# Forming the first expert pair's turned rows on the tensor engine, with idle transposes ahead of them

## The reference, cut to what matters

```python
s = sigmoid(ht @ w_router)                      # 512 tokens, 32 experts in 4 groups
g_idx = argmax(top_k(sel, 2)[0].sum(-1))        # best group, then two experts in it
...
xb = x_pad[tok]                                 # the tokens of one expert
hid = silu(xb @ w1[e]) * (xb @ w3[e])           # 1024 -> 512
ys = (hid @ w2[e]) * wt[:, None]                # 512 -> 1024
out = zeros.at[row_tok].add(ys)
```

## Time and profile before

| | |
|---|---|
| median of 3 runs | 800.81 us (800.76 to 807.31) |
| the profiled execution | 801.7 us |
| its span | 799.8 us |
| TensorE busy | 707.7 us (88%) |
| VectorE busy | 310.2 us (39%) |
| DMA engines, mean over the span | 327 GB/s, 261.22 MB |
| mean granted TensorE clock | 0.951 |

### The profile page before, as it was taken

One profiled execution on the slowest core, in us unless ns is written; L12 is line 12 of the kernel. 1 busy time (PEld: TensorE's weight loads), 2 busy tenths in 40 slices (PEclk: granted clock), 3 DMA queues, 4 the chain that ended last, 5 costly groups with the idle time before them and its releaser, 6 DMA issues.

```text
span 799.8 us, 9109 instructions
## 1 busy us (share of the span) xinstructions
PE 707.7 (88%) x3786; PEld 380.9 (48%) x3786; DVE 310.2 (39%) x555; ACT 176.2 (22%) x308; POOL 71.7 (9%) x68
## 2 busy tenths in 40 slices
PE   1899999796996589999976999999999998998994
PEld 0478778355685334434422444434444443453442
DVE  1172371479566522233304233333333323322326
ACT  4143362424134211101110011101101110110104
POOL 0007500119002010000000000000000000000000
PEclk9999999998898669999987899999999999999998
DMA  9990333896027919999998599999999999999972
GB/s 342 388 377 33 106 106 105 322 386 238 2 107 272 384 30 420 430 425 419 403 429 351 207 399 425 428 426 427 426 429 425 425 426 427 427 425 428 428 306 105
DMA packets 38857, 261.22 MB, mean 327 GB/s; under 512 B 4002, under 2 KB 4386, under 8 KB 26016
## 3 DMA queue, kind: packets, MB, share of 16 engines
q1 hardware_dynamic: 34560, 250.64, 76.5%
q0 software_dynamic: 2480, 6.16, 2.1%
q10 hardware_dynamic: 1776, 3.84, 1.3%
HBM read 260.76 MB, written 4.20 MB: 331 GB/s over the span
## 4 chain that ended last, share of the span: by engine, by line
PE 49%; DMA 12%; DVE 5%; ACT 1%; issue 1%; DVEq 0%; SPq 0%
PE bank L819 23%; DMA ring<-in_w 12%; PE bank L828 11%; PE bank L836 3%; PE bank L837 2%; PE bank L808 2%; DVE x L1492 1%; PE bank L793 1%; PE bank L811 1%; PE bank L860 1%; PE bank L801 1%; PE bank L845 1%; PE bank L869 1%; DVE x L1589 1%; PE bank L758 1%
## 5 line engine op out<-in xcount | busy, mean ns | idle before, releaser
L819 PE MATMUL bank<-ring,low 128*64 128x512 f32 x1024 | 231.8, 607 | 13.7 <-DMA ring<-in_w 10.8
L819 PEld LDWEIGHTS bank<-ring,low 128*64 128x64 f32 x1024 | 77.7, 140 | 158.0 <-issue 156.9
L1492 DVE TENSOR_TENSOR x<-x,bank 128x512 f32<-128x512 f32 x136 | 84.1, 681 | 84.5 <-PE bank L837 83.7
L828 PE MATMUL bank<-ring,low 128*64 128x512 f32 x512 | 113.4, 595 | 0.9 <-DVE x L1492 0.9
L828 PEld LDWEIGHTS bank<-ring,low 128*64 128x64 f32 x512 | 36.2, 137 | 66.1 <-issue 64.4
L1482 DVE SCALAR_TENSOR_TENSOR y_raw<-bank,keep,g2b 128x512 f32<-128x512 f32 x32 | 24.0, 751 | 88.4 <-PE bank L828 88.4
L1660 POOL DMA_INDIRECT xg_rows<-x_rows,keep x16 | 16.3, 1019 | 440.4 <-PE bank L793 423.2
L836 PE MATMUL bank<-y_hi,slot_tok 128*128 128x512 f32 x128 | 53.8, 420 | 0.2 <-DVE y_lo L1487 0.2
L1542 DVE TENSOR_TENSOR low<-low,bank 128x512 f32<-128x512 f32 x16 | 11.0, 687 | 110.1 <-PE bank L819 110.1
L1246 DVE TENSOR_TENSOR w_lo<-ring,w_hi 128x512 fp32r<-128x512 f32 x48 | 33.4, 712 | 51.8 <-ACT w_hi L1033 51.8
L837 PE MATMUL bank<-y_lo,slot_tok 128*128 128x512 f32 x128 | 50.6, 395 | 0.0
(11 more groups left out here) (242 smaller groups left out, 817.0 us busy)
## 6 DMA issues: line engine op xcount, KB each, us to landing
ring<-in_w SPq DMA_DIRECT2D x99, 2048.0 KB, 20.9
ring<-in_w_mod SPq DMA_DIRECT2D x12, 2048.0 KB, 15.2
ring<-in_w_in SPq DMA_DIRECT2D x4, 2048.0 KB, 22.5
ring<-in_w_out SPq DMA_DIRECT2D x2, 2048.0 KB, 12.7
x<-in_x SPq DMA_DIRECT2D x4, 512.0 KB, 6.4
after<-in_b_mod POOLq DMA_DIRECT2D x1, 2048.0 KB, 8.3
x_rows<-mid ACTq DMA_DIRECT2D x4, 512.0 KB, 15.4
out<-x SPq DMA_DIRECT2D x4, 512.0 KB, 2.6
```

The source lines that it names most:

```text
L819: last = mm(bk[e * CAP:(e + 1) * CAP, :], xb[:, k, e * CAP:(e + 1) * CAP], unit(n % SLOTS, KD)[:, k, :], start=k == 0, stop=k == KD - 1)
L828: last = mm(bk[e * CAP:(e + 1) * CAP, :], hid_t[:, k, e * CAP:(e + 1) * CAP], unit(n % SLOTS, KF)[:, k, hf * 512:(hf + 1) * 512], start=k ...
L1492: return v.tensor_tensor(acc[:, t, c], acc[:, t, c], bk[:, :], ALU.add)
```

## The change

`first_rows_turned` multiplies, for each of the eight pieces k and each token tile t, the piece of `h2` (stationary, every eighth column) by `onehot` (moving) and adds over t in PSUM. The result is what `turn_rows` would leave in G0 and G1 for pair 0: rows picked and transposed at once. It is placed after `p_ready` 1 and before `slots_to_partitions` of pair 0. `turn(0)` and gather 0 go; the gathers start with pair 1 and their counts shift by one. `keep_busy(n)` issues n transposes of `ident` into the bank of job hT20, whose contents have been read: 24 before TensorE waits for `chosen`, 8 before it waits for `p_ready` 1.

```diff
@@ -766,7 +766,16 @@
             logits(NT - 2)
             logits(NT - 1).then_inc(job_done, 1)
 
+            idle_bank = bank[JOB["hT20"] % 8]
+            assert len({JOB[n] % 8 for n in ("hT20", "lg", "rk", "cnt")}) == 4
+
+            def keep_busy(n):
+
+                for _ in range(n):
+                    nc.tensor.transpose(idle_bank[:, 0:P], ident, ident)
+
             b = start("rk")
+            keep_busy(24)
             pe.wait_ge(chosen, 1)
             for t in range(NT):
                 for u in range(t + 1):
@@ -878,17 +887,28 @@
             def turn(q):
-                pe.wait_ge(gath, 16 * q + 16)
+                pe.wait_ge(gath, 16 * q)
                 turn_rows()
 
+            def first_rows_turned():
+
+                for k in range(KD):
+                    g = (G0, G1)[k // 4]
+                    for t in range(NT):
+                        by_k = h2[:, t, :].rearrange("s (p k) -> s k p", k=KD)
+                        last = mm(g[:, (k % 4) * P:(k % 4 + 1) * P], by_k[:, k, :], onehot[:, t, :], start=t == 0, stop=t == NT - 1)
+                    if k % 4 == 3:
+                        last.then_inc(turned, 1)
+
             pe.wait_ge(moe_init, 1)
+            keep_busy(8)
             pe.wait_ge(p_ready, 1)
+            first_rows_turned()
             slots_to_partitions().then_inc(pt_psum, 1)
             pe.wait_ge(p_ready, 2)
             pe.wait_ge(pt_ready, 1)
             pe.wait_ge(w_ready, 1)
             slots_to_partitions().then_inc(pt_psum, 1)
-            turn(0)
@@ -1653,9 +1673,9 @@
             pool.wait_ge(rows_zero, 1)
             pool.wait_ge(h2_saved, 16 * NT)
-            for q in range(PAIRS):
+            for q in range(1, PAIRS):
                 pool.wait_ge(w_ready, q + 1)
-                if q > 0:
+                if q > 1:
                     pool.wait_ge(turned, 2 * q)
```

## The result

| | median, us | ratio to before, 95% interval |
|---|---|---|
| before | 802.82 (4 runs) | |
| changed | 815.84 (813.46 to 818.50, 4 runs) | 1.0155 [1.0096, 1.0214] |
| changed, timed again in more rounds | 816.96 (6 runs; before beside it 802.41) | 1.0187 [1.0137, 1.0237] |

The change makes the kernel slower by 13 to 15 us. The forecast of 808.1 (+7.3 us) had the sign right and about half of the size.

The account below looks back on a forecast made before the run. Expert weight loading bounds the last third, and pair 0's start shifts the end one to one. Idle transposes 0.75, block 8.6, slot products -2.1 sum to +7.3 us: 808.1 us, likeliest case 805.6 to 810.3, range 804.0 to 812.5.

Parts of the forecast that it names:

- a delay of pair 0 is carried one to one: Expert weight loads: each microsecond pair 0 starts later frees ring slot 0 later and ends the program a microsecond later.
- Rival D: Expert loads after pair 0: the delay is swallowed because the DMA engines are full from 299 us; 800.8 us, chance 0.05.
- The gather is worth nothing, its copies stay hidden: Before pair 0: removing gather 0 and its turn gains 0, as the lists end as late; ScalarE's copies stay behind them.
- 64 instructions: New block on TensorE: 32 plain float32 products, each two instructions.
- Their price: New block: 0.113 us per instruction at full clock, 0.21 at half; the block costs 8.6 us with the clock rising inside.
- The idle transposes 0.75 us late: Before the block: 8 idle transposes run until 277.7, past one-hot 0 at 276.83, adding 0.75 us.
- The clock at half before the ranks, and rising in the block: TensorE: half clock after 4.8 us idle before `chosen`, then full clock from 280.4, between 278.6 and 282.0.
- The two slot products at full clock, -2.1 us: `slots_to_partitions` 0 and 1, after the block: 1.47 us each instead of 2.50 and 2.53.
- Pair 0's first products, 0: Start of pair 0: TensorE idles through the lists, begins again at half clock, and the products cost 16.9 us as before.
- B: Rival: the clock does not rise in the block, slot products as slow as before; +14.4 us, 815.2, chance 0.08.
- A: Rival: idle transposes hold full clock through routing and pair 0 starts at full clock; +2.1 us, 802.9, chance 0.08.
- C: Rival: transposes don't count for the clock, so it rises about 282.0; +8.0 up to +8.8 us, chance 0.12.

Follow-up runs that it names:

- e1: The changed kernel with the stationary piece of h2 taken as 128 adjacent columns instead of every eighth; 809.04 us, ratio 1.0082 to before.
- e5: The changed kernel with the block adding over two of the four token tiles, 32 MATMULs instead of 64; 812.5 us, ratio 1.0107 to before.
- e9: The kernel of e5 timed in more rounds; 807.83 us, ratio 1.0073 to before.
- e10: The kernel before, gather kept, with idle transposes in TensorE's waits (56, 12, 16, 10) and two weight loads held until h2 is written; 795.37 us, ratio 0.9909.
- e4: The kernel before plus rows of measuring products and transposes at several operand strides ahead of the ranks, results unused; executed once for its profile, no time.
- e3: The kernel before with only the 24 and 8 idle transposes added; 805.07 us, ratio 1.0018 to before.
- e2: The changed kernel without the 24 and 8 idle transposes; 816.16 us, ratio 1.0134 to before.
- e6: The kernel before, gather kept, with idle transposes filling TensorE's waits (56, 12, 32, 6); 800.87 us, ratio 0.9972 to before.
- e8: The changed kernel as it is, timed again in more rounds; 816.96 us, ratio 1.0187 to before.

## Why the prediction was wrong

**What bounds the kernel, and that a delay of pair 0 is carried one to one: right.** From the end of pair 0's first products to pair 4's first it took 133.6 us before, 132.7 in the changed kernel, 133.3 to 133.5 in e1, e5 and e9, and from there to the end 361 to 363 us in all five. Rival D, that the loads swallow the delay, falls with that. One reading was loose: the clock line of the earlier trace rows shows six tenths in two slices of 20 us, a mean; that it falls to half is seen in the shorter stretches.

**The gather is worth nothing, its copies stay hidden: right.** Pair 0's first product followed the lists (`DVE keep L1550`) in the changed kernel too. It holds for the half clock of this routing: in e10, at full clock, the gathered rows came last and held pair 0.

**64 instructions: right. Their price: the step that failed.** "Price of one at full clock: L793, whose stationary operand has the same stride of 8 elements, takes 0.89 us for eight, 0.111 each ... I take 0.113." It was 0.237. I had two near rows: a transpose with this stride (L793), and a plain product with contiguous operands (L684). Each had one of the two properties and cost 0.11, and I took it that the two together would cost 0.11 as well. e4 shows they don't: the stride costs a plain float32 product double and a transpose nothing. I knew no row of the trace that had both properties at once, and my upper bound of 0.118 came out of the same kind of row, a transpose. The honest upper bound would have been wide here, and an underestimated block deserved more than the chance of 0.02 that I gave it. The block took 15.3 us instead of 8.6, +6.7.

The Trainium skill (Advanced Engine Details and Errata, SBUF Cachelines) says that an operand's accesses need at least two hits on a 16-byte line, or pay a penalty. e4 agrees: 8 bytes apart 0.12 us, 16 bytes apart 0.23. By that rule the block would have been suspect before any run. The Trainium skill (SBUF — State Buffer, Door 1: The DMA port swizzle) sets the limit at a stride of four float32; here four is already slow (0.23 us) and two (0.12) is the widest measured that is not, so the measurement decides.

**The idle transposes 0.75 us late: right** (0.75; in e3 0.74). **The clock at half before the ranks, and rising in the block: right.** It rose at about 282.1 us, 4.2 us after the idle transposes began, where I had 4.4. But the rise was worth nothing: the spacing was 0.240 us before it and 0.238 behind it.

**The two slot products at full clock, -2.1 us: wrong, -0.6.** They took 1.94 and 2.52 us. The second was at half clock, the +1.05 that I had among the bounds; within the first the clock fell, for which I had nothing. In e1, where the block's products came to stand 0.11 us apart, both were at full clock (0.89 + 0.66 us by rows). That points at the slow products as the cause, but does not show it. In e2 the same slow block was followed by a first slot product wholly at full clock, and in e4 some 17 us of such products left the clock at full until 315.2 us.

**Pair 0's first products, 0: nearly.** -0.9 us, at half clock for 4.1 us instead of 6.0. I had put up to -1.7 into the bounds.

Sum as measured: 0.75 + 15.3 - 0.6 - 0.1 (lists) - 0.9 = +14.4, against +7.3.

**Rivals.** B gave +14.4 us too, but by another mechanism: half clock all through. The clock was full for 13 of the block's 15 us, so B was wrong and its number came out by accident. A didn't happen, since 4.7 us stayed idle before the ranks. C can't be told apart by the block. But e6 and e10 speak against its rule. Before, the clock fell 3.0 us after the last router product. In e10 56 idle transposes stood behind that product, with hardly anything else on TensorE, and the clock fell only 13.1 us after it, at 278.9 us (columns: us; busy of PE, PEld, DVE, ACT, POOL; clock; DMA share; GB/s):

```profile
266.00:274.00 8.00, 6.74 (x73) 6.50 (x71) 6.93 (x43) 0.07 (x1) 0.00 (x0) 1.00 0.62 224
274.00:279.00 5.00, 3.29 (x46) 2.83 (x44) 2.47 (x12) 0.59 (x1) 0.74 (x1) 0.99 1.00 429
```

Full clock over the whole of the choice of experts, where before it was at half from 270 us on the earlier trace rows. Transposes in float32 did hold it here. The Trainium skill (TensorE: Matmul & The Clock Gate, Part 4, PE-mode transpose) says the contrary; in this case the measurement decides.

## What to carry to other kernels

When a new operation joins two properties that the trace has only apart (here a plain product and a stride of 32 bytes), the nearest rows do not bound it from above: measure it, or keep the range open. Here a float32 operand whose elements lay 16 bytes or more apart doubled the price of a plain product of 128x128 by 128 columns at full clock (0.23 us instead of 0.11), while a transpose took it for nothing; where that holds, let the transpose do the reordering. And before adding work in front of a queue, look what stands behind it: the gather that was removed was off the path, and the block that replaced it was put on it.

## What the runs showed of the hardware

- Plain float32 products of 128x128 by 128 columns start every 0.11 us at full clock with elements up to 8 bytes apart, and every 0.22 to 0.24 us with a stationary operand at 16, 32 and 64 bytes or a moving one at 32 bytes (e4; other shapes were not measured). At half clock the contiguous form takes 0.21 (e1). The strided one costs the same at either clock: 0.240 at half and 0.238 at full, in the changed kernel. Transposes take 0.11 to 0.12 at all of these strides.
- The granted clock can fall with no gap in the busy record. The changed kernel's TensorE was recorded as busy without a gap from 277.9 us, and the clock fell at 295.8 us within the small slot products; in e8 it did so at 293.9 us. With the block's products 0.11 us apart it stayed full through both slot products (e1). What made it fall is not shown.
- Idle transposes hold the clock when they fill the wait (e6, e10). They stand in TensorE's queue like any other work: in e6, with the clock at half for most of them, 32 took 4.9 us and held back the turn behind them.
